# Sums of weight blocks in an mLSTM branch: adding DMA transfers in place of GpSimd subtractions

## The reference

```python
proj = h @ w_in[l]
(qk_a, v_a, if_a, o_a, z_a, ...) = jnp.split(proj, cuts, axis=-1)
...
ha = mlstm_scan(qa, ka, va, i_pre, log_f)
ha = rms_norm(ha, mlstm_norm_g[l]).reshape(B, S, D_MLSTM).astype(dt)
y_a = ha * jax.nn.sigmoid(o_a) * jax.nn.silu(z_a)
```

## Time and profile before

| | |
|---|---|
| runs of the kernel before | 989.92, 989.94, 990.69 us; median 989.94 |
| the profiled execution's own time | 992.67 us |
| its span, first to last instruction | 990.8 us |
| TensorE, share of the span | 99% |
| DVE, ScalarE, GpSimd | 63%, 51%, 21% |
| mean granted TensorE clock | 0.998 |
| DMA read from and written to HBM | 94.39 MB, 4.19 MB |

### The profile page before, as it was taken

One profiled execution on the slowest core, in us unless ns is written; L12 is line 12 of the kernel. 1 busy time (PEld: TensorE's weight loads), 2 busy tenths in 40 slices (PEclk: granted clock), 3 DMA queues, 4 the chain that ended last, 5 costly groups with the idle time before them and its releaser, 6 DMA issues.

```text
span 990.8 us, 13870 instructions
## 1 busy us (share of the span) xinstructions
PE 982.6 (99%) x5013; PEld 862.5 (87%) x5013; DVE 620.9 (63%) x1029; ACT 509.1 (51%) x782; POOL 204.3 (21%) x150
## 2 busy tenths in 40 slices
PE   8999999999999999999999999999999999999998
PEld 6878888898989989989988888898998989888887
DVE  4878997779575464554656633885767757634352
ACT  5776644445444453543546222585766857641220
POOL 1000821221011011010110800352515325100000
PEclk9999999999999999999999999999999999999999
DMA  7724222122332323322332322606042052425321
GB/s 233 278 85 128 86 85 74 34 63 68 93 95 64 95 77 82 82 76 64 95 111 80 107 85 80 218 22 191 1 141 71 22 149 83 173 85 170 112 90 53
DMA packets 109262, 99.16 MB, mean 100 GB/s; under 512 B 4288, under 2 KB 94756, under 8 KB 108836
## 3 DMA queue, kind: packets, MB, share of 16 engines
q1 hardware_dynamic: 109204, 98.60, 32.3%
q10 hardware_dynamic: 16, 0.00, 0.0%
HBM read 94.39 MB, written 4.19 MB: 99 GB/s over the span
## 4 chain that ended last, share of the span: by engine, by line
PE 97%; ACT 1%; DVE 1%; DMA 1%; issue 0%; SPq 0%; ACTq 0%
PE proj L573 63%; PE proj L1007 9%; PE att L1034 6%; PE proj L1034 5%; PE att L880 2%; PE att L898 1%; PE att L820 1%; PE att L842 1%; PE proj L736 1%; PE att L888 1%; PE proj L964 1%; PE att L869 1%; DMA w_raw<-w_mem_kv_in 1%; PE att L977 0%; PE att L978 0%; PE att L979 0%
## 5 line engine op out<-in xcount | busy, mean ns | idle before, releaser
L1660 DVE TENSOR_TENSOR w_lo<-w_raw,w_hi 128x2048 fp32r<-128x2048 f32 (+1 forms) x66 | 141.3, 2140 | 149.0 <-ACT w_hi L1087 145.4
L1087 ACT ACTIVATE w_hi<-w_raw 128x2048 fp32r<-128x2048 f32 (+1 forms) x65 | 110.8, 1705 | 170.2 <-PE proj L573 168.6
L573 PE MATMUL proj<-hT_hi,w_hi 128*128 128x512 f32 x384 | 150.3, 391 | 1.2 <-DVE w_lo L2267 1.2
L573 PE MATMUL proj<-hT_hi,w_lo 128*128 128x512 f32 x384 | 149.8, 390 | 0.0
L573 PE MATMUL proj<-hT_lo,w_hi 128*128 128x512 f32 x384 | 149.6, 390 | 0.0
L573 PE MATMUL proj<-w_hi,hT_hi 128*128 128x384 f32 (+1 forms) x280 | 96.7, 345 | 0.0
L573 PE MATMUL proj<-w_hi,hT_lo 128*128 128x384 f32 (+1 forms) x280 | 95.3, 340 | 0.0
L573 PE MATMUL proj<-w_lo,hT_hi 128*128 128x384 f32 (+1 forms) x280 | 95.1, 340 | 0.0
L573 PEld LDWEIGHTS proj<-hT_hi,w_hi 128*128 128x128 f32 x384 | 72.1, 188 | 16.0 <-issue 1.5
L573 PEld LDWEIGHTS proj<-hT_hi,w_lo 128*128 128x128 f32 x384 | 72.1, 188 | 15.1
L573 PEld LDWEIGHTS proj<-hT_lo,w_hi 128*128 128x128 f32 x384 | 72.1, 188 | 14.5
(11 more groups left out here) (388 smaller groups left out, 2299.9 us busy)
## 6 DMA issues: line engine op xcount, KB each, us to landing
w_raw<-w_in_in SPq DMA_DIRECT2D x106, 256.0 KB, 3.2
w_raw<-w_in_in SPq DMA_DIRECT2D x32, 512.0 KB, 4.6
w_raw<-w_in_in SPq DMA_DIRECT2D x6, 1024.0 KB, 6.0
w_raw<-w_mem_kv_in SPq DMA_DIRECT2D x5, 1024.0 KB, 5.1
yF<-x_in SPq DMA_DIRECT2D x8, 512.0 KB, 7.3
w_raw<-w_branch_in SPq DMA_DIRECT2D x16, 256.0 KB, 3.5
w_raw<-w_branch_in SPq DMA_DIRECT2D x4, 1024.0 KB, 6.3
w_raw<-w_branch_in SPq DMA_DIRECT2D x8, 512.0 KB, 4.9
```

The costliest lines, as they stand in the source:

```text
L573: ins = mm(ps, lhs[a](k, k0), rhs[b](k, k0), start=(first and k == 0 and j == 0), stop=(last and k == KH - 1 and j == 2))
L1087: A_(w_hi[:, kh, :, 0:n], w_raw[:, kh, :, 0:n], ACT.Copy).then_inc(w_hi_done, 1)
L1660: V.tensor_tensor(w_lo[:, kh, :, 0:n], w_raw[:, kh, :, 0:n], w_hi[:, kh, :, 0:n].bitcast(F32), ALU.subtract).then_inc(w_lo_done, 1)
```

## The change

It does this:

- On the host a copy of the o, z, v columns of `w_in` is laid out by head and block (`w_units`), so that each of the four blocks of a head is 128 rows of 6 KB in one piece. The plain loads of a, b, c, d read from it, one transfer each, b ahead of a.
- Slot b holds W01, and GpSimd adds W00, then W11, then W10 to it with transfers that add at their destination (`accum_op`). These are operands 6, 7 and 10. Slot a is loaded a second time, with W01, once operand 4 is made (a new wait at the end of `load_head`), and gets W11 added: operand 9.
- The sums have plus signs throughout. So the signs move: the activation sum for one product is negated when it is split (a scale of -1 on ScalarE, a multiplication on DVE), two saved products are copied out negated, and DVE's adds become subtractions or stay, with operands swapped. The activation sums are made in another order, and products 2 and 3 take them in exchanged places.
- GpSimd's loop over the heads becomes a loop of the building program.
- The gate weights of the next section wait for operand 9 (first half) and operand 10 (second half), in place of all weight sums and operands 8 and 10.

```diff
+        def unit_rows(h, kh, half):
+            return w_units[bass.ds(h * (4 * P) + (2 * kh + half) * P, P), :]
...
-            def raw_block(dst, slot, parts, kh):
-                d3, at = dst.rearrange("p (k n) -> p k n", k=KH), 0
-                for c0, n in parts:
-                    sp.dma_start(d3[:, :, at:at + n], w_cols(wi, kh * KH, c0, n)).then_inc(raw_landed[slot], 16)
-                    at += n
+            def raw_block(dst, slot, h, kh, half):
+                sp.dma_start(dst, unit_rows(h, kh, half)).then_inc(raw_landed[slot], 16)
...
-                raw_block(raw_a, "a", left, 0)
-                raw_block(raw_b, "b", right, 0)
+                raw_block(raw_b, "b", h, 0, 1)
+                raw_block(raw_a, "a", h, 0, 0)
...
-                raw_block(raw_c, "c", left, 1)
+                raw_block(raw_c, "c", h, 1, 0)
...
-                raw_block(raw_d, "d", right, 1)
+                raw_block(raw_d, "d", h, 1, 1)
...
+                sp.wait_ge(op_low, h * OPERANDS + 5)
+                raw_block(raw_a, "a", h, 0, 1)
...
-            sp.wait_ge(t_done, 4 * A_HEADS)
-            sp.wait_ge(op_low, last + 8)
             for kh in range(2):
-                if kh:
-                    sp.wait_ge(op_low, last + 10)
+                sp.wait_ge(op_low, last + 10 + kh)
                 sp.dma_start(w_raw[:, kh], w_cols(wi, kh * KH, C_GATE, 512)).then_inc(w_landed[kh], 16)
...
-                unit_product(h, 2, h_sum(1), second_pair, True, lambda t: (bank_empty[2 + t], h + (AS[2][2 + t] + 1)))
+                unit_product(h, 2, h_sum(2), second_pair, True, lambda t: (bank_empty[2 + t], h + (AS[2][2 + t] + 1)))
...
-                unit_product(h, 3, h_sum(2), last_pair, False, lambda t: (u_saved, h * 6 + (t + 1)))
+                unit_product(h, 3, h_sum(1), last_pair, False, lambda t: (u_saved, h * 6 + (t + 1)))
...
-                return (raw_e, raw_f, raw_e, raw_f, raw_a, raw_c, raw_a, raw_a, raw_d, raw_b, raw_c)[n]
+                return (raw_e, raw_f, raw_e, raw_f, raw_a, raw_c, raw_b, raw_b, raw_d, raw_a, raw_b)[n]
...
-                elif n in (4, 5, 8):
-                    act.wait_ge(raw_landed["acxxd"[n - 4]], h * 32 + 32)
-                else:
-                    act.wait_ge(t_done, h * 4 + {6: 1, 7: 2, 9: 3, 10: 4}[n])
+                elif n in (5, 8):
+                    act.wait_ge(raw_landed["c" if n == 5 else "d"], h * 16 + 16)
+                elif n == 4:
+                    act.wait_ge(raw_landed["a"], h * 32 + 16)
+                elif n == 9:
+                    act.wait_ge(t_short, h * 16 + 16)
+                else:
+                    act.wait_ge(t_long, h * 48 + {6: 16, 7: 32, 10: 48}[n])
...
-                A_(s_parts[0][:, f], s_full[f], ACT.Copy).then_inc(s_high, 1)
+                A_(s_parts[0][:, f], s_full[f], ACT.Copy, scale=-1.0 if f == 1 else 1.0).then_inc(s_high, 1)
...
-                    V.tensor_tensor(buf[:, t], src[t][:, 0:UNIT_N], buf[:, t], ALU.add).then_inc(u_added, 1)
+                    V.tensor_tensor(buf[:, t], buf[:, t], src[t][:, 0:UNIT_N], op).then_inc(u_added, 1)
...
-            def weight_sum(dst, left, right):
-                for k in range(KH):
-                    at = slice(k * UNIT_N, (k + 1) * UNIT_N)
-                    ins = G.tensor_tensor(dst[:, at], left[:, at], right[:, at], ALU.subtract)
-                ins.then_inc(t_done, 1)
+            def add_block(dst, h, kh, half, done):
+                pool.dma_start(dst, unit_rows(h, kh, half), accum_op=ALU.add).then_inc(done, 16)
             def weight_sums(h):
-                pool.wait_ge(raw_landed["b"], h * 32 + 32)
-                pool.wait_ge(op_low, h * OPERANDS + 5)
-                weight_sum(raw_a, raw_b, raw_a)
-                pool.wait_ge(raw_landed["d"], h * 32 + 32)
+                pool.wait_ge(raw_landed["b"], h * 16 + 16)
+                add_block(raw_b, h, 0, 0, t_long)
                 pool.wait_ge(op_low, h * OPERANDS + 7)
-                weight_sum(raw_a, raw_d, raw_a)
-                weight_sum(raw_b, raw_d, raw_b)
-                pool.wait_ge(t_done, h * 4 + 2)
-                weight_sum(raw_c, raw_c, raw_a)
+                add_block(raw_b, h, 1, 1, t_long)
+                pool.wait_ge(raw_landed["a"], h * 32 + 32)
+                add_block(raw_a, h, 1, 1, t_short)
+                pool.wait_ge(op_low, h * OPERANDS + 8)
+                add_block(raw_b, h, 1, 0, t_long)
...
-            with pool.Fori(1, A_HEADS) as h:
+            for h in range(1, A_HEADS):
```

More of the change, by code:

```diff
@@ L141, in hybrid_block @@
                  mlstm_norm_g, dsa_q_norm_g, dsa_k_norm_g, mem_q_norm_g, mem_k_norm_g,
-                 w_mem_kv, w_branch, w_out, inv_freq, pos_cols, w_idx2, out):
+                 w_mem_kv, w_branch, w_out, inv_freq, pos_cols, w_idx2, w_units, out):
     ctx = ExitStack()
@@ L350, in hybrid_block @@
         op_high, op_low, op_used, u_done = sem("op_high"), sem("op_low"), sem("op_used"), sem("u_done")
-        t_done, u_saved, u_added, u_read = sem("t_done"), sem("u_saved"), sem("u_added"), sem("u_read")
+        u_saved, u_added, u_read = sem("u_saved"), sem("u_added"), sem("u_read")
+        t_long, t_short = sem("t_long"), sem("t_short")
         s_made, s_high, s_low = sem("s_made"), sem("s_high"), sem("s_low")
@@ L499, in load_head @@
             def load_head(h, first, last):
-                left = [(h * A_HD + C_OA, A_HD), (h * A_HD + C_ZA, P)]
-                right = [(h * A_HD + (C_ZA + P), P), (h * A_HD + C_VA, A_HD)]
                 sp.wait_ge(op_low, h * OPERANDS + 1)
@@ L1548, in a_body @@
                     act.wait_ge(proj_done[2], GB[2][2] + 4)
-                    sums_high(1)
+                    sums_high(2)
                 else:
@@ L1555, in a_body @@
                 if first:
-                    sums_high(2)
+                    sums_high(1)
                 operand_high(3, h, first)
@@ L1578, in a_body @@
                 operand_high(8, h)
-                unit_save(h, 2, (banks[2], banks[3]), u_fifth, 1)
+                unit_save(h, 2, (banks[2], banks[3]), u_fifth, 1, -1.0)
                 act.wait_ge(a_qk, h * 4 + 4)
@@ L1589, in a_body @@
                 operand_high(9, h)
-                unit_save(h, 3, last_half, u_second, 2)
+                unit_save(h, 3, last_half, u_second, 2, -1.0)
                 a_weights(h)
@@ L2208, in sums_low @@
             def sums_low(f):
-                dve.wait_ge(s_high, (4, 1, 2, 3)[f])
-                V.tensor_tensor(s_parts[1][:, f], s_full[f], s_parts[0][:, f].bitcast(F32), ALU.subtract).then_inc(s_low, 1)
+                dve.wait_ge(s_high, (4, 2, 1, 3)[f])
+                if f == 1:
+                    V.scalar_tensor_tensor(s_parts[1][:, f], s_full[f], -1.0, s_parts[0][:, f].bitcast(F32), ALU.mult,
+                                           ALU.subtract).then_inc(s_low, 1)
+                else:
+                    V.tensor_tensor(s_parts[1][:, f], s_full[f], s_parts[0][:, f].bitcast(F32), ALU.subtract).then_inc(s_low, 1)
             def a_body(h, first, last):
@@ L2225, in a_body @@
                 if first:
+                    sums_low(2)
                     sums_low(1)
-                    sums_low(2)
                 operand_low(5, h, first)
@@ L2241, in a_body @@
                 operand_low(8, h)
-                unit_add(h, 1, (banks[0], banks[1]), u_first, 2)
+                unit_add(h, 1, (banks[0], banks[1]), u_first, 2, ALU.add)
                 operand_low(9, h)
@@ L2368, in _ @@
             steps.then(ins)
-            steps.then(G.tensor_tensor(s_full[1], s_full[0], s_full[1], ALU.add))
             steps.then(G.tensor_tensor(s_full[0], s_full[2], s_full[0], ALU.subtract))
-            steps.then(G.tensor_tensor(s_full[2], s_full[1], s_full[2], ALU.subtract))
-            G.tensor_tensor(s_full[3], s_full[3], s_full[2], ALU.subtract).then_inc(s_made, 1)
+            steps.then(G.tensor_tensor(s_full[1], s_full[1], s_full[0], ALU.add))
+            steps.then(G.tensor_tensor(s_full[3], s_full[1], s_full[3], ALU.subtract))
+            G.tensor_tensor(s_full[2], s_full[1], s_full[2], ALU.subtract).then_inc(s_made, 1)
             def a_gate(h, half):
@@ L2428 @@
     arrays['w_idx2'] = np.ascontiguousarray(narrow.reshape(KT, P, I_COLS).transpose(1, 0, 2))
+    units = []
+    for h in range(A_HEADS):
+        o, z, v = (w[:, c + h * A_HD:c + (h + 1) * A_HD] for c in (C_OA, C_ZA, C_VA))
+        ozv = np.concatenate([o, z, v], axis=1).reshape(2, KH, P, 2, UNIT_N)
+        units.append(ozv.transpose(0, 3, 2, 1, 4).reshape(4 * P, KH * UNIT_N))
+    arrays['w_units'] = np.ascontiguousarray(np.concatenate(units, axis=0))
     for name, a in arrays.items():
```

6 lines of the change are left out of this document (3 added, 3 removed).

## The result

| | before | after |
|---|---|---|
| median of the runs on one chip (range, runs) | 990.32 us (989.92 to 991.45, 4) | 996.39 us (995.9 to 997.79, 4) |
| ratio of after to before, 95% interval | | 1.0062 [1.005, 1.0074] |
| the profiled execution's own time, its span | 992.67, 990.8 us | 996.58, 994.8 us |

What follows compares the result with a forecast made beforehand. TensorE, busy 982.6 of 990.8 us, was taken as the bound. First head 0.6, heads two to four 0.4 and the tail 0.4 us gave +1.4 us, 991.3 us on the 989.94 median; 8-in-10 range 989.2 to 998.5.

Steps and rivals of the forecast that it cites:

- no change that can be told: Whole kernel: a change within about 0.2%, 2.0 us; likeliest 991.3 us, chance 0.48.
- rival (a): Operand 7, all four heads: the adding transfer becomes the wait; 996.1 us at R = 8.5, 999.3 at 9.3; chance 0.38.
- R: Operand 7's adding transfer: time from GpSimd's issue to landing, taken as 7.3 us, between 4.4 and 9.3 us.
- What bounds the kernel; what leaves: Whole kernel: TensorE bounds it; GpSimd's 64 subtractions cost TensorE nothing, and slow DVE's low parts (2.00 us, 1.76 without).
- doubled bytes: Adding transfers: what lies in SBUF is read too, so 768 KB counts as 1536 KB at most, 7.0 us.
- Heads two to four: Operand 7 in the later heads: 7.17 us of cover against R of 7.3 us, 0.4 us lost in all.
- The first head allows 6.7 us: Operand 7, first head: cover for the adding transfer with DVE no longer slowed, so 0.6 us lost.
- Operands 6, 9 and 10 hidden: Their adding transfers have cover of 12.8, 12.9 and 15.7 less 3.3 us, so no stall.
- The tail: Gate-weight loads after the last head: the first now waits for operand 9's low part, 0.4 us; the second is hidden.
- Rival (b), contention before operand 6: Start of each head: SyncE's loads delay the first add, operands 6 and 7 slide; 996.1 us, chance 0.09.
- Can only shorten the plain loads: Plain loads: the copy's runs of 6 KB in place of 1 KB and 0.5 KB, named against contention before operand 6.
- the DMA engines are idle in that stretch of every head: Around operand 7's transfer: nothing shares the engines with it; named against its becoming the wait.

Runs made afterwards that it cites:

- e4: Changed kernel with GpSimd's 16 transfers as plain loads that no longer add, weight sums left out: 991.78 us.
- e13: Changed kernel, but in every head operand 9's adding transfer waits until operand 7's has landed: 1000.91 us.
- e9: Kernel before, with its plain loads from the copy laid out by head and block, one transfer each; GpSimd still subtracts: 990.76 us.
- e11: e8, with the second head's query loads held until operand 7's transfer has landed and block a's second load in their place: 991.45 us.
- e10: Changed kernel, but in the first head GpSimd waits for block c before issuing the first adding transfer: 1001.32 us, one run.
- e14: e11, with operand 9's adding transfer held in every head until operand 7's has landed: 997.71 us.
- e8: Changed kernel; in the first head DVE makes the two activation sums' low parts last and block c loads ahead of the 1 MB save: 995.42 us.
- e1: Changed kernel; in the first head DVE makes operand 6's low part ahead of the activation sums' low parts: 993.7 us.
- e2: Changed kernel; in the first head block c is loaded ahead of the 1 MB save of `merged`: 996.67 us.
- e12: Changed kernel; in the first head the two sums' low parts come last, query loads wait for operand 7's transfer, save stays put: 993.3 us.

## Why the prediction was right and wrong

The range (989.2 to 998.5) holds 996.4 us. The forecast, no change that can be told, was wrong: +0.62% is three times the bound of 0.2%. It came out as rival (a) by kind, with operand 7's transfer as the wait. That (a) also named 996.1 us is luck: its sum was R = 8.5 us in all four heads, and what happened was R = 7.3 us with one head that had half of the cover, and a slow clock behind it.

- **What bounds the kernel; what leaves.** Right. TensorE's wait is all that counts, and GpSimd's work was on no path. DVE's low parts take 1.76 us throughout.
- **The size of R, 7.3 us.** Right for the size: 7.0 in the first head, 6.7 to 6.9 in the later ones, on the same footing (issue to copy); counted from DVE's end, as the prediction counted, 7.3 in the first. The reason given for it, doubled bytes, fits the rates of e4 and e13. By the Trainium skill, DMA: Bandwidth & Descriptors, on the anatomy of one SWDGE DMA, the estimates were 3.8 us for the plain and 5.6 us for the doubled transfer. Measured were 4.7 and 6.6 to 7.0 us, so the measurement decides, and those estimates are about 1 us short on both.
- **Heads two to four, 3 x 0.13 us.** Right in kind, low by more than half: operand 7's product is 0.27 us longer in the second head, and the three heads lose 0.3, 0.5 and 0.2 us, 1.0 in place of 0.4.
- **"The first head allows 6.7 us."** This is the step that failed. It allowed 3.6. In place of 0.6 us the first head cost 5.6. The prediction took ScalarE's copy of operand 5 where it was before, 4.0 us ahead of operand 4's product, and only took back DVE's slowness. After, that copy starts 0.85 us ahead: 3.15 us later, and operand 6's low part is done 6.9 us past the start of that product, where the prediction had 3.8. The timelines split the 3.15 us into three parts. 0.9 of it is there in e9 already, where the lead is 3.1 us in place of 4.0: block a as one transfer, still in its old place. 1.3 more is there in e4 and e11, where ScalarE doesn't wait for block c and the lead is 1.8 us: these have block a behind block b. The last 0.9 is block c, which shares the engines with the save and with the first adding transfer, 15.1 us from issue to landing. In all of them ScalarE's own work from operand 4's copy to operand 5's takes 6.1 us, early block c or not, as e10 shows. No run put block a ahead again in the adding kernel, so that the 1.3 us are the swap's is read from the timelines, one profile each, and not tried. The prediction had held the new layout and the swapped loads for nothing.
- **The slow clock, 1.8 us.** Not in the prediction. It priced each wait at its length.
- **Operands 6, 9 and 10 hidden.** Right in the changed kernel. That they have cover and no more than cover, e10 (operand 6, 5.5 us) and e14 (operand 9, 1.4 us) show.
- **The tail, 0.4 us.** None: from the end of the last head's products to the gates it is 9.2 us before and after, and the 0.25 us of the last column are the fourth head's. ScalarE's copy of the gate weights is released by TensorE (0.33 us of idle time before it), as before. e13 and e14 show how near it was: with operand 9 later the gap grows by 1.0 and 1.4 us.
- **Rival (b), contention before operand 6.** Operand 6's transfer took 10.4 us in the first head, and ScalarE came for it 10.7 us after the issue (622.74 to 633.47), not the 12.8 of the later heads: no wait, by 0.3 us. Its second half, block c pushed back, happened and was worth 0.9 us, less than the 1.4 us of DVE's slack that it was given. "Can only shorten the plain loads" did not hold for block a in the first head: in e9 it is waited for by 2.0 us, where before it was there in time.
- **"Against (a): the DMA engines are idle in that stretch of every head."** False in the first head as soon as the order is mended (e8). The Trainium skill, DMA: Bandwidth & Descriptors, on issuing engines that are not separate queues, says that transfers of SyncE and GpSimd run on the same 16 engines and interleave. The trace agrees: 9.5 us with SyncE's loads ahead, 6.8 with four of them held (e8, e11).

What stays open: 1.0 to 1.2 us by which even e11 lies above before (0.4 us of it in the first head, 0.35 in the fourth, where operand 7's product starts 0.1 us late and takes 4.40 us); why block a lands later as one transfer; and what makes the clock fall behind some waits and not behind others.

## What to carry to other kernels

An adding transfer is a fair trade for an engine's additions only where its landing has 7 us of cover for 768 KB, and that cover has to be worked out for each head or stage apart: the first one, with its saves and first loads, had half of the others'. Where a new layout or a swap in the order of loads seems free, follow the first consumer of the load that came later, through all that its engine does next. And once such a transfer is the wait, look at what every queue puts on the engines just before it: holding back 1 MB that nobody needed yet was worth 2.9 us in the profiled stretch and 4.0 in the median (e11 against e8).

## What the hardware showed that I had not expected

- An adding transfer of 768 KB takes 7.0 us to land, a plain one from the same queue 4.7; GpSimd is busy for 0.85 to 1.07 us with each adding issue, and for 0.52 to 0.77 with a plain one (two in 1.04 to 1.08 us).
- A short wait of TensorE can cost more after it than during it. 3.8 us of idle time were followed by 3 us at clock 0.50 and a loss of 1.8 us; 0.7 us in e1 by a loss of 1.6; 2.8 us in e2 by 1.8. But 2.8 us in e8 and 2.2 in e12 were followed by none, so the length of the wait alone doesn't decide. Nor does the program: the profiled run of e8 has no fall behind its 2.8 us and a mean clock of 1.0, its four other runs have 0.998 or 0.997; e1 has 1.0 five times and 0.998 twice. One profile doesn't tell what such a wait costs, the mean clocks of all runs do.
- Two adding transfers issued one behind the other on GpSimd's queue cost the first of them 0.2 us at most (6.8 against 6.6), while plain loads from SyncE's queue ahead of one cost it 2.7 us (9.5 against 6.8).
